# Four matmuls of zeros behind each pair of slots in the expert retrieval of a decoder layer

## The reference

```
q = (xc @ w_query).reshape(PEER_CHUNK, PEER_HEADS, 2, PEER_HALF)
s = jnp.einsum('thcd,hckd->thck', q, keys)
top_s, top_i = lax.top_k(s, PEER_TOPK)
cand_s = top_s[:, :, 0, :, None] + top_s[:, :, 1, None, :]
best_s, best_j = lax.top_k(cand_s, PEER_TOPK)
gate = jax.nn.softmax(best_s, axis=-1)
act = gelu(einsum('thkd,td->thk', u_table[idx], xc))
return einsum('thk,thkd->td', gate * act, v_table[idx])
```

## Time and profile before

| | |
|---|---|
| time, median of 3 runs | 3442.51 us (3442.43 to 3445.3) |
| the profiled execution's own time | 3445.9 us |
| its span in the trace | 3444.1 us |
| mean granted clock of TensorE | 0.813 |
| TensorE busy (matmul) | 2338.2 us, 68% |
| VectorE busy | 2247.3 us, 65% |
| ScalarE busy | 1031.0 us, 30% |
| POOL busy | 1349.4 us, 39% |
| data moved by DMA | 1217.55 MB, mean 354 GB/s |

### The profile page before, as it was taken

How to read it: one execution, slowest core, us unless ns; L and a number is a source line. 1 busy time by engine, 2 the same in 40 slices (tenths; PEclk the granted TensorE clock), 3 DMA queues, 4 the chain that set the end, 5 groups by cost and what they waited for, 6 DMA issues and landing times.

```text
span 3444.1 us, 35081 instructions
## 1 busy us (share of the span) xinstructions
PE 2338.2 (68%) x9269; PEld 948.4 (28%) x9269; DVE 2247.3 (65%) x5256; ACT 1031.0 (30%) x3405; POOL 1349.4 (39%) x1241
## 2 busy tenths in 40 slices
PE   7997556575676657656765676567656855685676
PEld 4554443141132113211421142114111411151121
DVE  4433527879657855785578557856785577568754
ACT  2221213432332233233323332333233323433222
POOL 1231103434444444444444344444444444444432
PEclk9998778797798679867976897679768977896699
DMA  4212158999999999999999999999999999999998
GB/s 180 81 71 82 21 209 315 373 376 390 390 414 419 378 394 414 416 373 407 420 417 375 400 416 416 380 398 416 416 376 407 413 414 382 406 417 415 388 420 346
DMA packets 190131, 1217.55 MB, mean 354 GB/s; under 512 B 27112, under 2 KB 32664, under 8 KB 49176
## 3 DMA queue, kind: packets, MB, share of 16 engines
q0 software_dynamic: 157152, 1141.51, 82.1%
q1 hardware_dynamic: 30432, 71.87, 5.9%
q10 hardware_dynamic: 2312, 1.54, 0.2%
HBM read 1199.16 MB, written 15.55 MB: 353 GB/s over the span
## 4 chain that ended last, share of the span: by engine, by line
DMA 26%; PE 23%; DVE 20%; issue 11%; ACT 5%; POOL 1%; DVEq 0%; POOLq 0%; ACTq 0%; SPq 0%; PEldq 0%
DMA uv_ring<-in_uv_table,idx 26%; PE ACC L1968 14%; DVE uv_ring L1791 7%; PE TQ L1907 6%; DVE S L1710 2%; DVE idx_f L1711 2%; DVE S L1709 2%; PE OP L1888 2%; POOL uv_ring L1443 1%; ACT dg L1565 1%; ACT dot L1558 1%; PE TQ L1929 1%; PE ACC L1958 1%; ACT dot L1545 1%; DVE pos L1641 0%
## 5 line engine op out<-in xcount | busy, mean ns | idle before, releaser
L1968 PE MATMUL ACC<-uv_ring,dg 128*64 128x512 f32 x4352 | 1470.2, 787 | 954.0 <-ACT dg L1565 953.7
L1443 POOL DMA_INDIRECT uv_ring<-in_uv_table,idx x1088 | 1269.9, 1167 | 1730.3 <-PE ACC L1968 1395.6
L1791 DVE CUSTOM_DVE_ANT_0 uv_ring<-uv_ring,xn 128x1024 f32<-128x1024 f32 x1088 | 1321.4, 1226 | 732.6 <-DMA uv_ring<-in_uv_table,idx 663.1
L1968 PEld LDWEIGHTS ACC<-uv_ring,dg 128*64 128x64 f32 x4352 | 342.1, 166 | 1969.0 <-ACT dg L1565 1438.9
L1545 ACT ACTIVATE dot<-dot 128x2 f32<-128x2 f32 x544 | 110.8, 204 | 1755.8 <-DVE dot L1791 1755.4
L1565 ACT ACTIVATE dg<-stack,dot 128x64 f32<-128x64 f32 x1088 | 328.8, 341 | 48.1
L1558 ACT ACTIVATE dot<-gate,dot 128x1 f32<-128x1 f32 x1088 | 261.5, 287 | 18.2
L1907 PEld LDWEIGHTS TQ<-glu_and_queries,wq 128*128 128x128 f32 x2048 | 237.3, 194 | 63.7 <-issue 63.7
L1907 PE MATMUL TQ<-glu_and_queries,wq 128*128 128x128 f32 x2048 | 250.8, 281 | 0.0
L515 PE MATMUL PJ<-w_in,xT 128*128 128x512 f32 (+1 forms) x384 | 139.9, 523 | 3.2 <-DVE xT L401 3.2
L515 PEld LDWEIGHTS PJ<-w_in,xT 128*128 128x128 f32 x384 | 72.2, 190 | 70.3 <-issue 63.4
(11 more groups left out here) (338 smaller groups left out, 1709.7 us busy)
## 6 DMA issues: line engine op xcount, KB each, us to landing
uv_ring<-in_uv_table,idx POOLq DMA_INDIRECT x1088, 10.3
glu_and_queries<-in_w_glu SPq DMA_DIRECT2D x9, 1024.0 KB, 16.9
wq<-in_w_query SPq DMA_DIRECT2D x8, 1024.0 KB, 19.5
w_in<-in_w_in SPq DMA_DIRECT2D x8, 640.0 KB, 9.2
xt<-in_x SPq DMA_DIRECT2D x9, 512.0 KB, 4.7
xr<-scratch_x SPq DMA_DIRECT2D x9, 512.0 KB, 7.9
xc<-in_x_columns SPq DMA_DIRECT2D x8, 512.0 KB, 3.8
xk<-in_x SPq DMA_DIRECT2D x8, 512.0 KB, 3.5
```

The lines of the kernel that those rows point to most:

```text
L1443: pool.indirect_dma_start(out=ring[:, s_ % RING, :], out_offset=None, in_=a["uv_table"], in_offset=bass.IndirectOffsetOnAxis(ap=idx[:, s_: ...
L1791: V.tensor_tensor_reduce(row, row, xn[:, g, :], 1.0, 0.0, ALU.mult, ALU.add, dot[:, s_:s_ + 1]).then_inc(dots, 1)
L1968: ins = nc.tensor.matmul(ACC[GT * g:GT * (g + 1), b, :], dg[:, n % DG, :], ring[:, n % RING, D + 512 * b:D + 512 * b + 512], start=False, ...
```

## The change

A helper `add_nothing` issues `n` matmuls with the identity as weights and a column of zeros, broadcast to 128x128, as moving data; each adds zero to the first 128 columns of ACC's first bank. `retrieve` calls it with 4 behind each pair of slots of a prompt turn but the last pair, ahead of the preparation steps of these slots. The zeros are a new tile of one column, set by POOL at the start of its program; TensorE waits for that once at the start of its own.

```
@@ -1308,6 +1308,7 @@
+        zero = c.sb("zero", [P, 1])
@@ -1340,6 +1341,7 @@
+        zeroed = c.sem("zeroed_e")
@@ -1456,6 +1458,7 @@
+                pool.memset(zero[:], 0.0).then_inc(zeroed, 1)
                 retrieve("first", 0)
@@ -1971,10 +1974,17 @@
+                def add_nothing(n):
+
+                    for _ in range(n):
+                        nc.tensor.matmul(ACC[:, 0, 0:P], ident[:], zero[:].to_broadcast([P, P]), start=False, stop=False)
+
                 def retrieve(turn, t):
                     begin(t)
                     for b in range(0, slots_of(turn), BATCH):
                         add_v(t, b, 1 if turn == "samples" else GROUPS, b + BATCH == slots_of(turn))
+                        if turn != "samples" and b + BATCH < slots_of(turn):
+                            add_nothing(4)
@@ -1987,6 +1997,7 @@
+                pe.wait_ge(zeroed, 1)
                 pe.wait_ge(early, 48)
```

## The result

The changed kernel takes 3494.28 us (median of 4 runs, 3493.79 to 3499.81) against 3442.47 us for the kernel before: a ratio of 1.0154, 95% interval 1.0136 to 1.0171, so 52 to 53 us slower. The forecast had slower, with 3459 us and a range up to 3492. The sign is right; the size is three times too small.

What follows compares the result with a forecast made beforehand. The prediction took DMA to bound most heads, VectorE one, and dependences the turn's border. Its terms, 27 + 0 - 6 - 6 + 1.4 = +16 us, gave 3459 us against the median, range 3430 to 3492.

Steps and rivals of the forecast that it cites:

- the three regimes: Second phase: heads bound by DMA, one bound by VectorE, and a turn's border where a chain of dependences decides.
- the head of VectorE: Head 6 of a turn: VectorE's pace stays, clock up about half the time; -6 us (0 to -14).
- the border: Last pair of a turn, no addition behind it: warm in under half of the turns; -6 us (0 to -14).
- The price of an addition: TensorE, each group of eight added records: about 0.90 us at full clock.
- Light pairs: Pairs in heads like head 4: clock mostly up, no gain since DMA already moves 421 GB/s; 0.
- The w_bot heads: Head 1, sixteen records of L1888 behind two pairs: 0, at most +1 us a turn, 8 in all.
- Code: Instruction transfers: 8064 more instructions, 0.6 MB at 420 GB/s; +1.4 us.
- Dense pairs, the delay: Heads 2 and 3: ten pairs delay the next by 5.6 us if idle time fills, 9.0 if not; 5.6 taken.
- Dense pairs, the margin: Head 3: DMA queue hides 2.2 to 4.5 us before running dry; 2.2 taken, 3.4 us lost per turn.
- The sum: Whole kernel: 27 + 0 - 6 - 6 + 1.4 = +16 us; 3462 us by the profiled execution, 3459 by the median.
- The dense term: Heads 2 and 3: 3.4 us lost per turn, over eight turns +27 us (9 to 54).
- Rival B: Whole kernel: faster because the full clock pays; 3424 us by the median, 3433 with half of the excess gains; chance 0.25.
- Rival D: Light pairs: additions don't raise the clock, 5.5 us against 4.98; +160 us, 3600; chance 0.04.

Runs made afterwards that it cites:

- the border kernel: Against the kernel before: ten additions behind the last pair but one of each prompt turn, none elsewhere; ratio 0.9981 (0.9972 to 0.9991).

## Why the prediction was wrong

Its steps one by one.

*What bounds it, the three regimes.* Right. The loss comes from the place where TensorE had little idle time, the gains from the head of VectorE and the border, and the additions in heads 4 and 5 give nothing.

*The price of an addition*, 0.90 us for a group: measured 0.90, 6.53 less 5.63 us.

*Light pairs*, 0: right, by the kernel with heads 4 and 5 alone (1.0001), though the clock of head 4 is 0.85 in the changed kernel and not 0.9. *The w_bot heads*, 0: right, head 1 has 41.0 us for 41.1 in the mean of the steady turns. *Code*, +1.4 us: not seen apart. The queue q8 moved 1.92 MB for 1.39, 0.53 MB more where 0.6 were estimated, and the kernel with 50 of the 63 groups is faster than before.

*Dense pairs, the delay.* **This is the step that failed:** "If all is filled the delay is 5.6 us; if none [...] 9.0 us", of which it took 5.6. Two things were off. The run doesn't end at the pair of slot 56: the pairs of slots 58 and 60 follow it without a rest, the latter behind the scores, so twelve groups count, 10.8 us, and not ten. And of the run's idle time, 4.3 us before and 2.8 after in the mean, only 1.5 us was filled, not 3.45, since the waits are ScalarE's for queries that come later themselves. The text had named that coupling and then called filling the usual case. The measured delay is 9.7 us. (10.8 less 1.5 is 9.3; a group between two pairs without queries costs more, from slot 56 to 58 it is 2.96 us for 1.77.) The kernel with the additions behind the steps is the one that the forecast had priced: it fills the waits. That its cost, 1.0068 or 23 us, is near the +16 is in part luck: its run grows by 7.0 us where the forecast had 5.6, its dense heads lose 5.2 us a turn for 3.4, and its other heads give back 2.6 a turn for the forecast's 1.5.

*Dense pairs, the margin*, 2.2 us: right in size. The runs with 2, 4 and 8 additions absorb 1.4, 2.3 and 3.0 us, the change 1.7. The way to it was looser than the number. The gathers of head 3 in tile 3's turn of the changed kernel land in:

```profile
DMA to landing us min/median/max: 7.3/8.7/12.3
```

The least of this turn has hardly moved against 7.6 before. Over the six steady turns it is 5.8 to 7.8 us, where it was 7.4 to 8.6; with eight additions it is 5.3 to 6.5, down to the 5.4 of the earlier trace rows. But the rate of head 3 is 349 to 356 GB/s in all six turns of the change, also where the least landing is over 7 us. So the trace's least value is no measure of when the queue runs dry: the rate had fallen before it was reached.

*The head of VectorE*, -6 us: right in kind, 0.9972 is -9.6 us. *The border*, -6 us: 0.9981 is -6.5 us for ten additions there; the way was in part another (above). In the changed kernel the last pair is at 1.94 us in six of eight turns, where the forecast had fewer than half and gave as a sign that most would stay above 3 us.

*The sum*: 8 x 8.0 = 64 for the dense heads in place of 27. With the two gains as their own kernels measured them, -9.6 and -6.5 for -6 and -6, and +1.4, it is +49 us, against 52 measured. These two are borrowed: they were had with six and ten additions. In the changed kernel itself the other five heads gave back 1.2 us a turn, some 10 us, which makes +54. The dense term's high end, 54, lay below the measured 64, because the run had been cut at ten groups; so the range's top, 3492, came out 2 us short.

*Rival B*, faster because the full clock pays, is what the runs show in the two places where the clock can pay. It loses to the dense heads: with these alone the kernel loses 53 us, without them it gains 8. The rule of the Trainium skill that was set beside it ("TensorE: Matmul & The Clock Gate", Part 1), that activity releases the slow clock, is borne out: the mean clock went from 0.813 to 0.911 with the additions. *Rival D* didn't occur: with additions in heads 4 and 5 alone their pairs start 5.14 and 5.60 us apart in the mean of the steady turns, before 5.13 and 5.60.

## What to carry to other kernels

Filling work was free here only where the engine had idle time: look at the busy share by stage, and add nothing where the engine already runs back to back. Put filler behind the work that another engine waits for, not ahead of it; here that order alone was worth half the loss. A higher clock paid only outside the heads that the DMA bounds: with 13 of 63 groups left out the same idea gained 0.2%, and at two chosen places 0.5%.

## What was not expected of the hardware

Where the loop branches back, the next turn's first matmul came 6.2 to 6.6 us after the start of the last pair in four of five borders before (7.6 in one) and in all five after, whether that pair took 1.94 or 3.68 us; the idle time there is put down to "issue", 4.67 us of it in the row of the border kernel. The other kernels have a few longer ones, up to 8.1 us with two additions in the dense heads. What TensorE's sequencer does in this time no row shows. And additions of zeros raised the clock like other matmuls: 0.91 in VectorE's head with six behind each pair, where it had been 0.65.
